# Taking out two unused 64-byte gaps from the on-chip memory layout of a two-block fp32 model kernel

## What is computed

```
def swiglu(u, w1, w2):                       # four times, D_FF = 2816
    gate, up = jnp.split(u @ w1, 2, axis=-1)
    return (jax.nn.silu(gate) * up) @ w2

proj = u @ w_in                              # first block, mixer projections
proj = jnp.einsum('bsd,dc->bsc', h, w_in[layer])   # second block, 14 column groups
y_a = (silu(rg) * r_o) @ ret_w_out[layer]    # likewise hgrn_w_out, swa_w_out
mix = merged @ w_o[layer]
ff = swiglu_2(...) if layer % 2 == 0 else moe_swiglu(...)    # D_EXP = 3584, 8 experts, top 2
```

## Time and profile before

| | |
|---|---|
| time, median of 3 runs | 3172.99 us (3172.69 to 3173.51) |
| span of the profiled execution, first to last instruction | 3172.4 us |
| PE busy | 3136.1 us, 99% |
| weight loads busy | 2611.5 us, 82% |
| VectorE busy | 2219.9 us, 70% |
| ScalarE busy | 1871.5 us, 59% |
| mean DMA rate | 230 GB/s |

### The profile page before, as it was taken

How to read it: one execution, slowest core, us unless ns; L and a number is a source line. 1 busy time by engine, 2 the same in 40 slices (tenths; PEclk the granted TensorE clock), 3 DMA queues, 4 the chain that set the end, 5 groups by cost and what they waited for, 6 DMA issues and landing times.

```text
span 3172.4 us, 39857 instructions
## 1 busy us (share of the span) xinstructions
PE 3136.1 (99%) x15857; PEld 2611.5 (82%) x15857; DVE 2219.9 (70%) x2626; ACT 1871.5 (59%) x2487; POOL 48.8 (2%) x67
## 2 busy tenths in 40 slices
PE   9999999999999999999999999999999999999998
PEld 7888588888887878988888889887888888888887
DVE  5559865655445566665754757667999999999998
ACT  5442554544455444655544457465777777777777
POOL 1000000000000000000000000000000000000000
PEclk9999999999999999999999999999999999999999
DMA  9444274665536444535374545346999999999995
GB/s 326 145 168 145 92 234 150 201 204 166 140 107 219 146 160 160 186 134 185 124 235 138 181 161 194 123 153 226 384 376 382 382 376 382 382 376 382 381 377 225
DMA packets 383079, 730.39 MB, mean 230 GB/s; under 512 B 13027, under 2 KB 152689, under 8 KB 382784
## 3 DMA queue, kind: packets, MB, share of 16 engines
q1 hardware_dynamic: 376576, 705.87, 62.4%
q0 software_dynamic: 6224, 22.16, 2.3%
q10 hardware_dynamic: 112, 0.05, 0.0%
HBM read 720.16 MB, written 7.86 MB: 229 GB/s over the span
## 4 chain that ended last, share of the span: by engine, by line
PE 93%; DVE 4%; ACT 2%; issue 0%; DMA 0%; DVEq 0%; SPq 0%; ACTq 0%
PE duo L1075 14%; PE duo L1077 14%; PE duo L1076 14%; PE acc L1075 8%; PE acc L1077 8%; PE acc L1076 8%; PE aux L1075 2%; PE aux L1076 2%; PE aux L1077 2%; PE aux L553 1%; PE duo L554 1%; PE duo L553 1%; PE aux L554 1%; PE duo L555 1%; PE aux L555 1%; PE duo L398 1%
## 5 line engine op out<-in xcount | busy, mean ns | idle before, releaser
L1741 DVE TENSOR_TENSOR weights_split<-w,weights_split 128x1024 fp32r<-128x1024 f32 x672 | 792.5, 1221 | 80.2 <-ACT weights_split L1717 78.9
L1717 ACT ACTIVATE weights_split<-w 128x1024 fp32r<-128x1024 f32 x672 | 675.3, 1053 | 205.4 <-PE duo L1077 128.3
L1075 PE MATMUL duo<-weights_split,u_high 128*128 128x512 f32 x1776 | 698.7, 393 | 1.2 <-issue 0.8
L1077 PE MATMUL duo<-weights_split,u_low 128*128 128x512 f32 x1776 | 692.6, 390 | 0.0
L1076 PE MATMUL duo<-weights_split,u_high 128*128 128x512 f32 x1776 | 692.0, 390 | 0.0
L427 DVE TENSOR_TENSOR w_low<-w,w_high 128x1024 fp32r<-128x1024 f32 x304 | 368.2, 1223 | 291.0 <-ACT w_high L418 289.6
L1220 DVE TENSOR_TENSOR weights_split<-w,weights_split 128x1024 fp32r<-128x1024 f32 x320 | 377.2, 1221 | 268.4 <-ACT weights_split L1208 268.2
L418 ACT ACTIVATE w_high<-w 128x1024 fp32r<-128x1024 f32 x304 | 318.2, 1057 | 315.1 <-PE acc L1077 80.2
L1208 ACT ACTIVATE weights_split<-w 128x1024 fp32r<-128x1024 f32 x320 | 320.7, 1054 | 239.3 <-PE duo L1077 139.9
L1075 PEld LDWEIGHTS duo<-weights_split,u_high 128*128 128x128 f32 x1776 | 333.7, 188 | 71.6 <-issue 3.7
L1077 PEld LDWEIGHTS duo<-weights_split,u_low 128*128 128x128 f32 x1776 | 333.5, 188 | 70.2
(11 more groups left out here) (448 smaller groups left out, 4954.8 us busy)
## 6 DMA issues: line engine op xcount, KB each, us to landing
w<-in_ffn_w_dram SPq DMA_DIRECT2D x130, 1024.0 KB, 7.8
w<-in_moe_w_gate_dram SPq DMA_DIRECT2D x112, 1024.0 KB, 8.1
w<-in_moe_w_up_dram SPq DMA_DIRECT2D x112, 1024.0 KB, 7.9
w<-in_moe_w_down_dram SPq DMA_DIRECT2D x112, 1024.0 KB, 9.6
w<-in_w_in_dram SPq DMA_DIRECT2D x92, 1024.0 KB, 7.2
w<-in_hyb_w_in_dram SPq DMA_DIRECT2D x18, 1024.0 KB, 8.2
w<-in_ffn_w_gate_dram SPq DMA_DIRECT2D x11, 1024.0 KB, 7.6
w<-in_ffn_w_up_dram SPq DMA_DIRECT2D x11, 1024.0 KB, 10.1
```

The lines of the kernel that those rows point to most:

```text
L1075: pe.matmul(bank_out, x_hi, w_hi, start=first, stop=False, skip_group_check=True)
L1077: return pe.matmul(bank_out, x_lo, w_hi, start=False, stop=last, skip_group_check=True)
L1717: act.activation(units[:, place, 0, cut], src[:, cut], ACT.Copy).then_inc(sem("moe_high"), 1)
L1741: m = dve.tensor_tensor(units[:, place, 1, cut], src[:, cut], units[:, place, 0, cut], ALU.subtract)
```

## The change

The two unused tensors are no longer declared. `w_high` then begins at byte 65536, `h` and all that follows it 128 bytes earlier than before, and every tensor that a split product reads begins at 0 in its stretch of 512 bytes. No instruction is added, removed or moved.

```
         w_low = sb("w1_low", [P, RING, 4096], F32R)
-        sb("lead", [P, 16])
         with nc.sbuf_tensor("w2", [P, RING2, 2, D], F32) as w2:
             pass
         w_high = sb("w2_high", [P, PIECES, 1024], F32R)
-        sb("gap", [P, 16])
         h = sb("h", [P, NT, D])
```

## The result

The changed kernel took 3178.42 us in the median of 19 runs (3176.43 to 3180.92), the kernel before 3173.63 us in 19 runs beside it. The ratio is 1.0015, with a 95% interval from 1.0008 to 1.0022: 0.15% slower, by an interval that lies above 1, though by less than the 0.2% that the prediction counts as no change; 0.35% faster was forecast. Every time in this document is the median of the fast runs; one run with a gap of 192 bytes (3902 us) and one with 256 bytes (8179 us) were slow and are left out. The profiled execution has a span of 3176.8 us, 4.4 us more than before.

The account below looks back on a forecast made before the run. PE's matmul pace was taken as the bound; savings of 6.3, 1.8, 6.0 and 0.8 us made 14.9, cut to 11.9 for uneven starts and 11.1 for PE's 93% of the chain: 3161.9 us, 0.35% faster, range 3157 to 3182.

Parts of the forecast that it names:

- Units cost nothing: Unit matmuls keep their place relative to the activations, so stay at 226.7 ns: no change.
- Pieces with 512 columns go to the units' pace: Pieces in `pe_tm_piece` and `pe_block_rows` go from 230.8 and 228.9 to 226.7 ns: 8.1 us saved.
- the deduction for uneven starts: A fifth taken off the summed 14.9 us because the even pace isn't there at once, keeping 11.9 us.
- Turned pieces: 2400 turned matmuls of 256 columns go from 115.8 to 113.3 ns: 6.0 us saved.
- mixed pieces: 192 matmuls of 256 columns where roles alternate go from 117.5 to 113.3 ns: 0.8 us saved.
- The upper bound: Highest pace allowed for turned matmuls, 120 ns instead of 115.8: 10 us lost; not believed.
- The slow triple of 120 ns: Three mixed-piece matmuls of 256 columns taking 0.36 us in the profile before, used as the turned pace's upper bound.
- rival 1: 512 columns gain 6.5 us, turned and mixed matmuls at 120 ns lose 10.6: 3177 us, 4 us slower; chance 0.09.
- Rival 2: Turned and mixed matmuls lose 10.6 us, 512-column pieces gain nothing: 3184 us; chance 0.18, including unnamed losses.
- Rival 3: The place in 512 bytes doesn't set matmul pace, so nothing changes: 3173 us; chance 0.12.
- Rival 4: Only 512-column pieces gain, turned ones stay at 115.8 ns: 6 us saved, 3167 us; chance 0.17.
- Rival 5: VectorE becomes the bound in the experts, from 119 ns more per subtraction; chance 0.02.

Follow-up runs that it names:

- experiment 5: Against the changed kernel, units begin 64 bytes further than activations and pieces, which stay at 0: 3196.25 us, 1.0066.
- experiment 1: Kernel timing only fp32r matmuls, a load before each, at several operand distances and sixteen layouts; at equal places 226.7 ns for 512 columns, 120.0 for 256.
- experiment 2: Six kernels with the unused gaps removed singly or given other lengths, against the kernel before: from 3168.78 us (0.9982) to 3183.67 us (1.0029).
- H 192, A 192: Layout in the pace-only kernel: high pieces at byte 192, activations and units at 192, low pieces at 0; 232.1 ns at 512 columns.

## Why the prediction was wrong

- **The bound and its reading**: right. PE sets the end, and pace moved it, all but some 0.5 us of clock. 93% of the chain is PE in both. The clock of 9 tenths or more in every slice didn't show the short fall at 803 us, as a slice is 79 us long.
- **Units cost nothing**: right, 227.3 ns in the mean in both, and experiment 5 shows why.
- **Pieces with 512 columns go to the units' pace**: right, 226.7 ns in both ways of feeding. The term was 8.1 us and 6.5 after the deduction for uneven starts; it measured 6.1.
- **Turned pieces: the step that failed.** "A matmul of 256 columns that pays only what columns pay takes 113.3 ns. I take that, being the value to which both lead." One argument halved the 226.7 ns of 512 columns, and with them an excess that doesn't halve; the other took the difference between 512 and 256 columns, in which a fixed excess drops out. The excess is 13.3 ns for each matmul at equal places with 256, 320, 384 or 512 columns (experiment 1): 120.0 ns. The term was -6.0 us and measured +8.7, or +9.5 at one clock. The mixed pieces took the same wrong step, -0.8 forecast and +0.5 measured.
- **The upper bound was the true value.** The slow triple of 120 ns was put aside because "no row with a load before each matmul comes near it". It was itself such a row, and 226.7 - 213.3 = 13.3 ns, worked out in the prediction, added to 106.7 gives 120.0. That sum wasn't made. "Unlike with 512" in rival 1 was no reason either: the excess at equal places is the same.
- **Rival 1 came true**, with its two signs and nearly its price: 10.6 us lost against 6.5 gained there, 9.2 and 6.1 measured, 10.0 and 6.1 at one clock. It had a chance of 0.09. What was held against it, that this pace needs alternating roles, was wrong; turned pieces among themselves run at 120.0 ns. Its own reason, that the load has no time in which it runs alone, isn't shown by any run.
- **Rival 2** has the loss without the gain and falls with the 226.7 ns of the pieces. **Rival 3** falls with every row of the table in experiment 2. The Trainium skill, "TensorE: Matmul & The Clock Gate", Part 2, first step, says that the load has a port of its own and doesn't steal read bandwidth; the pace of matmuls with a load before each depends all the same on the distance of the two operands, 113.3 to 120.0 ns at 256 columns and 226.7 to 236.7 at 512. Why is not shown by any run. **Rival 4** had the turned pace unchanged. **Rival 5** and the other engines: right, 1221 and 1223 ns and idle time of 79.9 and 293.8 us.
- **Not in the prediction**: the lower clock, 1.7 us of the profiled span of after in the router stage and 1.2 us of that of before at 803 us. That the first belongs to the layout isn't shown. It came at this stage in every changed layout that ran and not in the one profiled execution of before, but moving a matmul only moved it. What decides it stays open, as does what decides between 113.3 and 117.8 ns at 192 bytes.

The net of before to after, at one clock: turned +9.5, pieces with 512 columns -6.1, mixed +0.5, units +0.2, the lower clock +1.7 and -1.2, all else -0.2: +4.4 us, as in the spans. The medians differ by 4.8.

## What to carry to other kernels

When a kernel is bound by fp32r matmuls with a load before each, measure the pace for each shape at several distances between the begin of the streamed and of the stationary operand before choosing a layout: the distance that is best for 512 columns is the worst for 256. Measure the products in the order in which the kernel has them, since mixed distances don't average. Don't scale an excess from one width to another without a second width that shows whether it grows with columns; take off the columns first and look at what is left. Equal places are a plausible rule and were the wrong one here; a gap of 192 bytes, found by a table of sixteen layouts, was worth 0.18%, with an interval from 0.08 to 0.27%.

## What the runs showed of the hardware

- The pace of fp32r matmuls with a load before each depends on the distance of the two operands' begins modulo 256 bytes, as long as the distance stays the same. Against equal places the other distances cost up to 10.0 ns more at 512 columns (236.7 at 240 bytes) and up to 6.7 ns less at 256; at 320 columns distances of 0, 64, 128 and 192 take the same.
- Where the distance changes from matmul to matmul, the pace isn't the mean of the paces at each: 232.1 ns against 227.4 (H 192, A 192, 512 columns).
- At equal places each pays 13.3 ns over its columns at 256, 320, 384 and 512 columns; 128 columns take 111.6 ns, 58.3 over theirs. The Trainium skill, "TensorE: Matmul & The Clock Gate", Part 1, "Wait — 56ns, not 53.3ns?", gives about 2.5 ns for a warm matmul; here fp32r with a load before each stays above that everywhere (6.7 ns at the least), while each of the two matmuls that the trace has for one in plain fp32, 429.2 ns at 512 columns, is two times 213.3 and 2.5.
- One sequence of operands can keep one of two paces for a whole stretch of 96 matmuls and more, 113.3 or 117.8 ns, and the same stretch of the program had one pace in one profiled execution and the other in another.
